# First feed-forward projection of a two-block transformer kernel: from three 256-column matmuls to a 512-column and a 256-column matmul for each weight block

## The reference, cut to what matters

```python
def rms_norm(x, gain):
    y = xf * lax.rsqrt(jnp.mean(xf * xf, axis=-1, keepdims=True) + RMS_EPS)
    return (y * gain.astype(jnp.float32)).astype(x.dtype)
...
        h = rms_norm(x, ffn_norm_pre[layer])
        up = jnp.einsum("bsd,df->bsf", h, w_up[layer])
        up = causal_dwconv(up, conv_f_w[layer], conv_f_b[layer])
        gate, val = jnp.split(up, 2, axis=-1)
        ffn_out = jnp.einsum("bsf,fd->bsd", jax.nn.gelu(gate) * val, w_down[layer])
        x = x + rms_norm(ffn_out, ffn_norm_post[layer])
```

## Time and profile before

| what | value |
|---|---|
| median of 3 runs | 1142.52 us (1142.43 to 1142.56) |
| the profiled execution's own time | 1142.97 us |
| its span, first to last instruction | 1141.1 us |
| PE busy | 1130.6 us (99%) |
| DVE busy | 870.1 us (76%) |
| ACT busy | 665.0 us (58%) |
| POOL busy | 383.0 us (34%) |
| mean DMA rate | 179 GB/s |

### The profile page before, as it was taken

One profiled execution on the slowest core, in us unless ns is written; L12 is line 12 of the kernel. 1 busy time (PEld: TensorE's weight loads), 2 busy tenths in 40 slices (PEclk: granted clock), 3 DMA queues, 4 the chain that ended last, 5 costly groups with the idle time before them and its releaser, 6 DMA issues.

```text
span 1141.1 us, 23482 instructions
## 1 busy us (share of the span) xinstructions
PE 1130.6 (99%) x8304; PEld 1039.8 (91%) x8304; DVE 870.1 (76%) x1364; ACT 665.0 (58%) x1127; POOL 383.0 (34%) x387
## 2 busy tenths in 40 slices
PE   9999999999999999999999999999999999999997
PEld 9999999989999999899979988888888898888886
DVE  6968897987699888448877787777666877777753
ACT  6687657655576666446557665555555555555453
POOL 3468000602246664222000344445220025444431
PEclk9999999999999999999999999999999999999999
DMA  7676434676355556653645365557655445556662
GB/s 263 192 216 209 134 116 131 202 240 209 128 184 185 184 184 182 202 188 103 194 148 168 111 188 186 190 188 261 205 188 182 147 135 180 186 187 190 204 204 78
DMA packets 56851, 204.55 MB, mean 179 GB/s; under 512 B 6881, under 2 KB 7305, under 8 KB 56657
## 3 DMA queue, kind: packets, MB, share of 16 engines
q1 hardware_dynamic: 54576, 196.96, 54.6%
q0 software_dynamic: 1920, 6.28, 1.9%
q10 hardware_dynamic: 288, 0.39, 0.1%
HBM read 200.95 MB, written 2.63 MB: 178 GB/s over the span
## 4 chain that ended last, share of the span: by engine, by line
PE 95%; DVE 3%; ACT 1%; issue 1%; DVEq 0%; ACTq 0%
PE bank L1643 26%; PE bank L1644 15%; PE bank L1649 13%; PE bank L1650 13%; PE bank L1651 13%; PE bank L1646 3%; PE bank L1777 2%; PE bank L1779 2%; PE bank L1778 2%; PE bank L1697 1%; DVE w_lo L856 1%; PE bank L1880 1%; PE bank L1870 1%; PE bank L1747 1%; PE bank L1902 1%
## 5 line engine op out<-in xcount | busy, mean ns | idle before, releaser
L856 DVE TENSOR_TENSOR w_lo<-raw,w_hi 128x1024 fp32r<-128x1024 f32 x370 | 465.8, 1262 | 113.4 <-ACT w_hi L351 108.5
L351 ACT ACTIVATE w_hi<-raw 128x1024 fp32r<-128x1024 f32 x370 | 389.4, 1054 | 137.7 <-PE bank L1644 59.8
L1649 PE MATMUL bank<-h_two,w_hi 128*128 128x256 f32 x1072 | 310.2, 289 | 0.7 <-ACT work L487 0.3
L1650 PE MATMUL bank<-h_two,w_hi 128*128 128x256 f32 x1072 | 303.2, 283 | 0.0
L1651 PE MATMUL bank<-h_two,w_lo 128*128 128x256 f32 x1072 | 303.2, 283 | 0.0
L1643 PE MATMUL bank<-h_two,w_hi 128*128 128x512 f32 x714 | 257.8, 400 | 0.2 <-DVE h_two L887 0.2
L1644 PE MATMUL bank<-h_two,w_lo 128*128 128x256 f32 x816 | 212.7, 281 | 0.0
L1649 PEld LDWEIGHTS bank<-h_two,w_hi 128*128 128x128 f32 x1072 | 205.4, 192 | 4.6 <-issue 2.9
L1650 PEld LDWEIGHTS bank<-h_two,w_hi 128*128 128x128 f32 x1072 | 205.5, 192 | 0.6
L1651 PEld LDWEIGHTS bank<-h_two,w_lo 128*128 128x128 f32 x1072 | 205.4, 192 | 0.0
L1643 PE MATMUL bank<-u_two,w_hi 128*128 128x512 f32 x574 | 203.5, 397 | 0.0
(11 more groups left out here) (256 smaller groups left out, 1601.5 us busy)
## 6 DMA issues: line engine op xcount, KB each, us to landing
raw<-in_stream SPq DMA_DIRECT2D x372, 512.0 KB, 3.6
u_two<-u_two POOLq DMA_DIRECT2D x4, 384.0 KB, 5.7
bias_rows<-bias_row POOLq DMA_DIRECT2D x1, 1536.0 KB, 15.1
work<-in_x_t SPq DMA_DIRECT2D x2, 512.0 KB, 5.4
work<-in_x_t POOLq DMA_DIRECT2D x1, 1024.0 KB, 6.3
work<-bias_rows POOLq DMA_DIRECT2D x1, 1024.0 KB, 9.7
work<-bias_rows POOLq DMA_DIRECT2D x1, 512.0 KB, 5.7
out<-work SPq DMA_DIRECT2D x2, 256.0 KB, 2.5
```

The costliest lines, as they stand in the source:

```text
L351: A(w_hi[:, slot, :], raw[:, slot, :], ACT.Copy).then_inc(hi_ready, 1)
L856: v.tensor_tensor(w_lo[:, slot, :], raw[:, slot, :], w_hi[:, slot, :].bitcast(F32), ALU.subtract).then_inc(lo_ready, 1)
L1649: mm(out, w_hi[:, slot, s], r_two[:, 0, :], start=start, stop=False)
L1650: mm(out, w_hi[:, slot, s], r_two[:, 1, :], start=False, stop=False)
```

## The change

The 44 tiles of the loop take the wide form. ScalarE copies the upper half of each tile's bank (`low_half`) as soon as the tile is done, and waits for the second tile of the pair ahead of the convolution's copies instead of behind them. VectorE's eviction of a tile becomes two instructions: bank plus `LOW` into `UB`, then, after a wait for that very sum (a new semaphore, `up_added`), `UB` times `RSTD` in place. The counts of `low_out` for the later stages move by the 44 copies.

```diff
+        up_added = sem("up_halves_added")
...
-        for name, n_tiles in (("pb", C), ("pa", C - 1), ("down", C - 1), ("up1", 2 * F2), ("down1", C - 1),
+        for name, n_tiles in (("pb", C), ("pa", C - 1), ("up", 2 * F1 - 4), ("down", C - 1), ("up1", 2 * F2), ("down1", C - 1),
...
                     if not first:
                         multiplied(PART["up"] + 2 * p, i, 4)
+                        low_half(TILE["up"] + 2 * p)
                         hi(i, 4, PART["up"] + 2 * p + HI_AHEAD)
+                        multiplied(PART["up"] + 2 * p + 1, i, 4)
+                        low_half(TILE["up"] + 2 * p + 1)
                     act.wait_ge(evacuated, lin(i, 4, TILE["up"] + 2 * p + 2))
                     act.wait_ge(pair_free, lin(i, 2, p + 1))
                     for j in (2 * p, 2 * p + 1):
                         A(YB[:, j, :], UB[:, j, :], ACT.Identity, scale=dcol("fconv_w", i * 4 + (2 * 2 * F1 + j)),
                           bias=dcol("fconv_b", i * 4 + j)).then_inc(u_conv, 1)
                     if not first:
-                        multiplied(PART["up"] + 2 * p + 1, i, 4)
                         hi(i, 4, PART["up"] + 2 * p + 1 + HI_AHEAD)
...
                 for j in (2 * p, 2 * p + 1):
-                    multiplied(PART["up"] + j, i, 4)
-                    normed(UB[:, j, :], TILE["up"] + j)
+                    if isinstance(i, int):
+                        multiplied(PART["up"] + j)
+                        normed(UB[:, j, :], TILE["up"] + j)
+                    else:
+                        dve.wait_ge(low_out, lin(i, 4, LOW_BEFORE["up"] + j + 1 - 4))
+                        v.tensor_tensor(UB[:, j, :], out_of(TILE["up"] + j), LOW[:, (TILE["up"] + j) % BANKS, :],
+                                        ALU.add).then_inc(up_added, 1)
+                        dve.wait_ge(up_added, lin(i, 4, j + 1 - 4))
+                        v.tensor_tensor(UB[:, j, :], UB[:, j, :], RSTD, ALU.mult).then_inc(evacuated, 1)
...
                 tile(0, c + 3, t + 3)
-                tiles(c + 4, t + 4, n - 4)
+                tiles(c + 4, t + 4, n - 4, wide=norm == "ffn")
```

## The result

The changed kernel takes 1150.95 us (median of 4 runs, 1150.78 to 1152.43) against 1142.53 us before (4 runs beside them): the ratio is 1.0076, with a 95% interval of 1.0064 to 1.0087. It is slower by 8.4 us; 9.9 were predicted, and the time lies within the range (1146.0 to 1160.5 us). Its profiled execution took 1150.93 us, with a span of 1149.1 us.

What follows compares the result with a forecast made beforehand. VectorE was taken to become the bound at 6.11 us a pair (5.18 + 0.93) against TensorE's 5.64; with the start's 1.35 us and the slack at the end, 9.9 us later: 1152.4 us median, range 1146.0 to 1160.5.

Steps and rivals of the forecast that it cites:

- The bound: In the 44-tile loop VectorE, at 6.11 us a pair against TensorE's 5.64, becomes the bound from the first pair on.
- TensorE's 2.6 us: 44 wide tiles, each 0.06 us shorter than narrow ones: all that can be gained, only while TensorE remains the bound.
- The scaling's price: On VectorE, scaling starts 0.46 us behind its sum; a pair's evictions take 1.60 us instead of 0.67, adding 0.93.
- GpSimd's interference: Delay to VectorE per pair: some 0.1 us at the first scaling, some 0.55 at `lo`; 0.65 found, 0.67 kept.
- ScalarE's cover: ScalarE's Gelu, copy, `hi`, copy take some 2.1 us where VectorE needs 2.33, so they are covered by 0.2 us.
- The loop's start: No trailing `lo` covers ScalarE's copies there: 1.35 us late, once, moving the first pair's end from 331.57 to 332.92.
- One sign that did not come: In the stage's profile after, TensorE idle 0.2 to 0.3 us a tile before the tile's first weight load.
- The end: 21 more pairs at 6.11 us end at 461.23 against 450.19, 11.0 us later.
- The wait for the last product: Behind the down-projection's first tile, TensorE waits once, over 2 us, for L1214.
- The last block: Of the down-projection's first tile: starts at 463.44 instead of 453.53, 9.9 us later, and everything behind it moves too.

Runs made afterwards that it cites:

- copies first: The changed kernel with ScalarE making both copies of a pair ahead of its rounding of the next weight part: 1151.66 us, ratio 1.0078.
- pair scaling: The changed kernel, all 44 tiles wide, with one scaling of 512 columns for each pair instead of two: 1153.46 us, ratio 1.0093.
- both edits together: The changed kernel with one scaling for each pair and both of ScalarE's copies ahead of its rounding: 1150.62 us, ratio 1.0073.
- the narrow kernel with two scalings: The kernel before, narrow matmuls and no ScalarE copies, with a second, dependent multiplication behind each of the 44 evictions: 1151.76 us, ratio 1.0076.
- the half-wide ones: The change for one pair of each turn: first pair 1141.44 us, repeated 1141.46; second pair 1141.92; first pair with one scaling 1142.78.
- three of four wide: The change for three of the four tiles of each turn, the fourth keeping the narrow form: 1147.03 us, ratio 1.0032.

## Why the prediction was right

*The bound.* TensorE's 2.6 us could be had (scaling left out: all of it), and VectorE's load stood in the way. The scaling's price, 0.46 us behind its sum and 1.60 us for a pair, was measured as 0.44 to 0.45 and 1.67 with a delay of 0.1 in it.

*GpSimd's interference.* The placing was right in each of its three parts: some 0.1 us at the first scaling (0.52 against 0.42), the rounding beside the second sum, 0.55 at the `lo` (1.76 against 1.21). I had kept 0.67 in place of the 0.65 so found; that, and sums 0.44 to 0.45 ahead of their scalings where I took 0.46, make 6.11 instead of 6.07. The run without the subtraction shows that it is the cause of the 0.55. That the product is the cause of the 0.1 is read from its place alone; no run takes it away.

*ScalarE's cover* of 0.2 us: right, and as thin as said. It is gone as soon as VectorE is quicker (0.21 us of waiting without the scaling).

*The loop's start.* 332.92 predicted for the second pair, 332.67 measured. The late second sum had one good side that I had not seen. In this first pair GpSimd's rounding (327.16 to 327.63) ran for the most part in VectorE's wait and its subtraction (327.81 to 328.55) beside the second sum and the scaling, which took 0.67; the first `lo` took 1.21, not 1.76.

*One sign that did not come.* TensorE was to be idle 0.2 to 0.3 us in each tile. It is idle once a pair, some 0.5 us, for the first `lo`; the second one is done before TensorE asks for it. The sum does not use this.

*The end.* 21 pairs and the start give 461.23 by the prediction, 460.21 by the trace (the 0.25 at the start, 0.8 from the period). The wait for the last product was put at over 2 us; it is 2.08. The last block starts at 462.40, 8.87 us later than at 453.53, where 9.91 were predicted.

*What lies elsewhere.* Of these 8.87 the span keeps 8.0. Nearly all of the rest is regained at one place of the second mixer, which the change doesn't touch: TensorE's small matmuls (L1978) broke off there before, and don't after. Their train starts 8.82 us later than before (at 582.02 and 590.84), and the matmul behind it 8.01 (583.52 and 591.53).

```profile
583.15 0.45 PE L1978 MATMUL bank<-work 128*32 128x32 f32 x29 [0.62 <-issue]
```

That row is of the kernel before; after, all 64 of the group stand in one row:

```profile
590.84 0.77 PE L1988 MATMUL bank<-work 128*32 128x32 f32 x64
```

What makes the gap was not tried. It is absent in five of the eleven other profiles (without the scaling, without the subtraction, copies first, pair scaling, and both edits together); the narrow kernel with two scalings, the half-wide ones and three of four wide have 0.3 to 0.5 us of it. Its absence is why the kernel without the scaling gave 1139.2 us and not 1139.9. So of the 1.5 us between the predicted 1152.4 and the measured 1150.95, 1.0 is in the period and the start; what is regained behind the stage gives 0.9 more, and 0.4 go the other way, as the profiled execution of before was 0.45 over its median and that of after is at its own.

## What to carry to other kernels

Before work is moved to a second engine, add up that engine's period with the first one's pace beside it: here the gain was 0.12 us a pair, the room on VectorE 0.46 (5.18 beside TensorE's new 5.64), and the price 0.93. The idle time of the steady loop before, 0.67, overstates that room. Where the room doesn't do for all of a loop, it may do for a part: two wide tiles in four fit into both engines' pace and won 0.1%, three lost. And in this kernel a VectorE instruction with two operands in SBUF was not priced by its own time alone: 0.5 to 0.8 us of delay a pair stayed with VectorE wherever GpSimd's three instructions fell, and most of it went only when the subtraction was left out. Count the instructions beside which such work fits.

## What the runs showed of the hardware that was not expected

A single wait of 2 us changed TensorE's clock in some executions. In the pair-scaling kernel, behind the wait for the last product, which is as long (2.06 us) as in the changed kernel (columns: start:end, length, engines' busy times, PE clock, DMA share, GB/s):

```profile
460.00:464.00 4.00, 1.94 (x9) 1.48 (x8) 2.71 (x5) 3.40 (x4) 0.00 (x0) 0.86 0.70 242
464.00:468.00 4.00, 4.00 (x18) 3.41 (x18) 2.66 (x4) 1.43 (x3) 1.53 (x1) 0.72 0.54 188
468.00:472.00 4.00, 4.00 (x25) 3.55 (x24) 1.45 (x2) 2.03 (x2) 0.00 (x0) 1.00 0.66 225
```

and in the changed kernel, profiled:

```profile
460.00:464.00 4.00, 1.92 (x11) 1.42 (x10) 2.71 (x5) 3.77 (x6) 0.00 (x0) 1.00 0.59 197
464.00:468.00 4.00, 4.00 (x25) 3.48 (x24) 3.15 (x4) 1.45 (x2) 1.53 (x1) 1.00 0.77 252
```

The granted clock falls to its lower level (1.2 GHz) for a time behind the wait in the one, and 18 matmuls are done in 4 us instead of 25. The profiled executions of the narrow kernel with two scalings and of the three-of-four kernel show the same (0.84 and 0.73 in the stretches from 460 and 464 us, 0.75 and 0.82 from 456 and 460), those with the copies first do not. In the two-scalings and the three-of-four kernel the first matmuls behind the wait still ran at the pace of the full clock (0.35 us for a block of 512 and 256 columns, 0.60 to 0.64 from 462.68 and 458.11 on), so the fall came while TensorE was at work again. By the Trainium skill (page "TensorE: Matmul & The Clock Gate", section "What's actually happening") throttled is the default state, and activity releases it. The traces agree in that the fall came behind the one long wait and the full clock came back under steady work. They don't show why waits of 2.08 and 2.12 us (changed kernel, copies first) left the clock alone and one of 1.94 (three of four) did not.

The times go with it. Three of four wide: 1145.33 and 1145.55, and 1147.03 to 1147.36, the profiled one with the lower clock being of the second group; two scalings on narrow tiles: 1150.65 and 1150.99, and 1152.54 and 1152.95, again with the profiled one in the second; copies first (profiled at 1151.00) and both edits together (1149.89) have full clock and are of the first group of theirs. All four executions of the pair-scaling kernel, 1153.40 to 1153.58, lie by its profiled one, so probably all had the low clock. The traces have the price by itself: an addition on VectorE some 60 us later (L910; L908 and L913 in the others) starts at 524.08 in the changed kernel, at 526.30, 524.93 and 519.83 in the pair-scaling, the two-scalings and the three-of-four kernel. Against the last operand of each, that is 1.6, 1.7 and 1.6 us more than in the changed kernel. So the low clock costs some 1.6 us, and the one run of the changed kernel at 1152.43 us is likely such a one; it has no profile of its own, so this is a conclusion from the times. The kernel without the subtraction, which waits there for 0.5 us, shows no such groups (1139.54 to 1140.16). The prediction had no price for the clock behind its one long wait.
